# Triangular inverse of layer 0: which parts of a product are evicted and by which engine, where the memory heads stand, and where four gate panels stand

## The chip, the cores and the metric

One core of one Trainium2 chip runs the whole program. The metric is the device time of one execution in microseconds (us), the median of several. Engines in what follows: PE is TensorE (matmuls), DVE is VectorE, ACT is ScalarE, POOL is GpSimd, SP is SyncE, which only issues the loads of the weights. Each engine takes its instructions strictly in the order in which the program lists them, and waits at a semaphore when an operand isn't there yet.

## The reference, cut to what matters

Two blocks run one after the other on 256 tokens of width 1024. The change touches only layer 0 of the first block:

```python
proj = h @ a_w_in[i]                       # 29 panels of 128 columns: z, gate, q_mem, g_mem
y_br = rwkv7_time_mix(z, ...)              # 12 heads of 64, a scan over the tokens:
def step(state, inp):
    sa = jnp.einsum('bhvk,bhk->bhv', state, -kk_t)
    state = (state * w_t[:, :, None, :]
             + sa[..., None] * (kk_t * a_t)[:, :, None, :]
             + v_t[..., None] * k_t[:, :, None, :])
    y_t = jnp.einsum('bhvk,bhk->bhv', state, r_t)
def memory_cross_attention(q, mem_n, w_mem_kv):     # 4 heads of 64, 256 memory rows
    s = jnp.einsum('bshd,bmhd->bhsm', q, k) * (HEAD_DIM ** -0.5)
    p = jax.nn.softmax(s, axis=-1)
    o = jnp.einsum('bhsm,bmhd->bshd', p, v)
y = jnp.concatenate([y_br * jax.nn.silu(gate), y_mem * jax.nn.silu(g_mem)], axis=-1) @ w_out[l]
x = x + rms_norm(y, post_norm[l])
```

The rest (layer 1, two feed-forward parts, retention, sparse attention) is the same in both kernels.

## The kernel before, in words

A Python function `schedule()` writes one list of steps by hand; each engine's program walks that list and emits its own part of each step, so the order of the list is the order on every engine. Weights come as panels of 128 output columns. A panel is split into a high part (`w_hi`, ACT, line 1422) and a low part (`w_lo`, DVE, line 1758) and multiplied in 24 matmuls (lines 2281, 2282, 2284); the splits run two panels ahead of the matmuls. `between` is a list of panels and small steps from which `fill()` takes the next one at places written into the schedule. A panel's eviction is listed when the next panel is. For a gate panel the eviction is a sigmoid on ACT (line 1412) and a product on DVE (line 1819).

The scan of layer 0 is done in two chunks of 128 tokens. It needs the inverses of 24 unit triangular 128x128 matrices (12 heads, 2 chunks), kept as six groups of four. Their 32x32 diagonal blocks are inverted by substitution on DVE, one row at a time over 30 steps (`lane`, lines 1850 and 1854), after a transposition (`lanes_in`) and before another (`lanes_out`, line 1867). ACT then scatters the blocks into `xt_all` in four copies of 32 partitions (line 1524). Two levels (block sizes 32 and 64) follow for each group g, in `invert(g)`:

- `tri_1`: DVE transposes the group's diagonal blocks into `work` (line 1871)
- `tri_y`: PE multiplies (line 2339), DVE multiplies the whole 128x512 product by a mask table m5 or m6 (line 1875)
- `tri_x` (first level only) and `tri_t`: PE multiplies (line 2351), DVE adds the whole 128x512 product to the operand (lines 1881 and 1886)

`skewed` interleaves several such generators: in each round every live one makes one move, and one more joins. The groups go in two passes of three. Ahead of the first pass stand the four masked products `mat(0, "ak")` (PE line 2383, DVE line 1904); behind it `step_w(0)` (line 2400); behind the second `mat(1, "ak")`, `step_u(0)` (line 2410), and so on: state, `step_y(0)` (lines 2421, 2423), `step_w(1)` (lines 2397, 2400), `step_u(1)`, then `fill(5)` with five gate panels, `step_y(1)`, three group norms (lines 1923 to 1927), and the four memory heads. A memory head is `mem_a` (scores on PE line 2463; maximum, negation, reciprocal and two scalings on DVE lines 1934 to 1942; two exponentials on ACT line 1560), `mem_b` (four transpositions on PE line 2474, copy on ACT line 1567) and `mem_c` (two matmuls on PE line 2483, product with the gate on DVE line 1950). Its buffers lie in `xt_all`, which the inverse uses until `step_u(1)`, and its exponentials wait for `step_y(1)`. Then `branch0` splits the operands of the output projection (ACT 1580, 1583; DVE 1957) and `mix_out(0)` begins (panels `w_out`).

Of the kernel before, what the change touches and what calls it, by code (L numbers as in the profile page):

```python
# [8 lines left out]
P = 128  # L9
# [7 lines left out]
BT = BR // P  # L17
HD = 64
# [80 lines left out]
for _name, _n in VECTORS:  # L99
# [5 lines left out]
            ("dist", 384), ("mid", 2)]  # L105
TABLES_R = [(n, P) for n in ("neg_up", "m5", "m6", "up", "upinc", "cen")]
TABLES_B = [("rcos", T), ("rsin", T), ("acos", T), ("asin", T), ("icos", T), ("isin", T), ("decay", RET_HEADS * KW),
# [33 lines left out]
def const_tables():  # L141
# [10 lines left out]
    m = {"neg_up": (c > r) * -1.0, "up": (c > r) * 1.0, "upinc": (c >= r) * 1.0}  # L152
    for j in (5, 6):
        n = 1 << j
        m[f"m{j}"] = ((r // (2 * n) == c // (2 * n)) & (r // n > c // n)) * 1.0
    m["cen"] = a["ident"] - a["blkm"]
# [110 lines left out]
def build(nc, xT, memT, metaT, vecs, tab_a, tab_r, tab_b, lora, w, outT):  # L267
    with ExitStack() as ctx:
# [52 lines left out]
        xt_all = sb("xt_all", [P, 6, 512], ph)  # L321
        mrs = sb("mrs", [P, MEM], ph)
        inner = ExitStack()
        mh, ml = sb("mh", [P, KT, S], inner, F32R), sb("ml", [P, KT, S], inner, F32R)
# [18 lines left out]
        st1_flat = sqr_flat[:, 2 * BR:2 * BR + BT * HD]  # L343
        quarter = [xt_flat[:, i * 512:(i + 1) * 512].rearrange("p (a b) -> p a b", a=2) for i in range(4)]
        mp0, mpt0 = quarter[0:2], quarter[2:4]
        ybuf0 = tiles8(work_flat[:, 0:2048])
# [56 lines left out]
        def tabr(name):  # L403
            o, n = OFF_R[name]
            return tr[:, o:o + n]
# [29 lines left out]
        col_first = lambda a: a.rearrange("p a c -> p c a")  # L435

        def slot(g):
            o = 3072 + (g % 3) * 1024
            return work_flat[:, g * 512:(g + 1) * 512], work_flat[:, o:o + 512], work_flat[:, o + 512:o + 1024]
# [13 lines left out]
        def mats(c, kind, p, half):  # L453
# [22 lines left out]
            "keys_by_pool", "a_inv", "mod", "k_tilde", "bonus_r", "bonus_in", "bonus_lnb", "r_hat", "bonus_gated", "gate_scaled")  # L476
        nlt_d, ln_in, ln_m, ln, ln_out, xx_d, yy_d, xt_d = steps_of(
            "inverse_by_vector", "nlt", "lanes_in", "lane_product", "lane", "lanes_out", "x", "y", "t")
        blk_d, xts = steps_of("inverse_by_scalar", "block", "scattered")
        nl_mm, y_mm, x_mm, t_mm = steps_of("inverse_by_tensor", "l", "y", "x", "t")  # L480
# [58 lines left out]
        def schedule():  # L539
# [344 lines left out]
            def invert(g):  # L884
                do("tri_1", g)
                for level in (5, 6):
# [430 lines left out]
        def gpsimd_program(g):  # L1317
            on = Lane(g)
            for kind, *a in steps:
# [9 lines left out]
                elif kind == "zero":  # L1329
                    on.wait_ge(*in_lo.past(("h0", KT - 1)))  # L1330
                    g.memset(blocks[:, 24:BLK, :], 0.0).then_inc(*blk_zero.up(0))
                    g.memset(xt_flat, 0.0).then_inc(*xt_zero.up(0))
                elif kind == "key_b":
# [59 lines left out]
        def scalar_program(s):  # L1393
# [22 lines left out]
            for kind, *a in steps:  # L1416
# [102 lines left out]
                elif kind == "lanes_out":  # L1519
                    on.wait_ge(*ln_out.past(0))  # L1520
                    on.wait_ge(*xt_zero.past(0))
                    for r in range(P // BLK):
                        o = slice(r * BLK, (r + 1) * BLK)
                        s.activation(xt_flat.rearrange("p (m c) -> p m c", m=24)[o, :, o], blocks[o, 0:24, :],
                                     ACT.Copy).then_inc(*xts.up(r))
                elif kind == "v_tok":
# [24 lines left out]
                elif kind == "mem_a":  # L1551
# [190 lines left out]
        def vector_program(v):  # L1742
# [9 lines left out]
            for kind, *a in steps:  # L1752
# [112 lines left out]
                elif kind == "lanes_out":  # L1865
                    on.wait_ge(*ln.past(BLK - 2))
                    v.transpose(col_first(blocks), col_first(lanes)).then_inc(*ln_out.up(0))
                elif kind == "tri_1":
                    g, = a
                    on.wait_ge(*xts.past(P // BLK - 1))  # L1870
                    v.transpose(slot(g)[1], xt_all[:, g, :]).then_inc(*xx_d.up((g, 4)))
                elif kind == "tri_y":
                    g, level, b, freed = a
                    on.wait_ge(*y_mm.past((g, level)))
                    v.tensor_tensor(v4(slot(g)[2]), v4(banks[b][:, :]), b4(tabr(f"m{level}")), ALU.mult).then_inc(
                        *yy_d.up((g, level)))
                elif kind == "tri_x":
                    g, level, b, freed = a
                    xx = slot(g)[1]
                    on.wait_ge(*x_mm.past((g, level)))  # L1880
                    v.tensor_tensor(xx, xx, banks[b][:, :], ALU.add).then_inc(*xx_d.up((g, level)))
                elif kind == "tri_t":
                    g, level, b, freed = a
                    xt = xt_all[:, g, :]
                    on.wait_ge(*t_mm.past((g, level)))
                    v.tensor_tensor(xt, xt, banks[b][:, :], ALU.add).then_inc(*xt_d.up((g, level)))
                elif kind == "bonus_b":
# [5 lines left out]
                elif kind == "mat":  # L1893
# [3 lines left out]
                    if (c, which) == (0, "ak"):  # L1897
                        on.wait_ge(*xts.past(P // BLK - 1))
# [9 lines left out]
                elif kind == "state":  # L1908
                    ba, f_a, bb, f_b = a
                    on.wait_ge(*st_mm.past(0))  # L1910
                    for i in range(BT):
                        on.wait_ge(*ed_e.past(i))
                        for p in range(2):
                            o, at = HD * p, (i % 3) * P + HD * p
                            last = v.tensor_scalar(st1[o:o + HD, i, :], banks[bb if i > 2 else ba][o:o + HD, at:at + HD],
                                                   ed[o:o + HD, i, 0, CH:CH + 1], math.exp(-MID), ALU.mult, ALU.mult)
                        last.then_inc(*st_d.up(i))
# [343 lines left out]
        def tensor_program(pe):  # L2261
# [7 lines left out]
            for kind, *a in steps:  # L2269
# [71 lines left out]
                elif kind in ("tri_x", "tri_t"):  # L2341
# [3 lines left out]
                    on.wait_ge(*yy_d.past((g, level)))  # L2345
                    on.wait_ge(*(xt_d.past((g, level - 1)) if level > 5 else xts.past(P // BLK - 1)))
                    after(on, freed)
# [359 lines left out]
```

## Time and profile before

| | us |
|---|---|
| median of 3 runs | 1418.23 |
| lowest, highest | 1412.1, 1421.2 |
| the profiled execution's own time | 1421.38 |
| its span, first to last instruction | 1419.6 |

The profiled execution is another one than the three runs. What lies around its span is 1421.38 - 1419.6 = 1.8 us. The mean granted clock of TensorE over the span is 0.945 of 2.4 GHz. Read the table as the total to which savings inside the span are applied one for one, if they lie on the chain that sets the end.

### The profile page before, as it was taken

How to read it: one execution, taken by the hardware profiler on the slowest of the kernel's cores; microseconds unless marked ns; L12 is line 12 of the kernel's file. 1: busy time of each engine (PE TensorE's matmuls, PEld its weight loads, DVE VectorE, ACT ScalarE, POOL GpSimd, SP SyncE). 2: the span in 40 equal slices, each digit the busy share in tenths (PEclk: the TensorE clock that was granted, in tenths of full speed). 3: DMA queues.
4: the chain of work that ended last, by engine and by line, in shares of the span. 5: the costliest groups of instructions: out<-in, count | busy, mean ns of one | idle time of the engine just before them, and what ended most of it. 6: DMA issues, size and time to landing. Idle time of an engine off the chain costs nothing.

```text
span 1419.6 us, 23796 instructions
## 1 busy us (share of the span) xinstructions
PE 1290.4 (91%) x9682; PEld 1222.2 (86%) x9682; DVE 867.4 (61%) x1490; ACT 621.2 (44%) x1059; POOL 163.3 (12%) x165
## 2 busy tenths in 40 slices
PE   6979489968799788999998999989999998999997
PEld 6978377838689588999998999878999998999997
DVE  5668753334666557666547774657845656767652
ACT  5765101234445546444433333544344544645441
POOL 3126000400000101221002200001400000122200
PEclk9999699878899889999999999989999999999999
DMA  6433100203144236555542553324545434655561
GB/s 244 144 118 105 45 1 16 75 0 119 59 139 130 89 117 203 194 173 164 174 130 94 185 167 119 104 76 135 180 163 177 141 127 151 213 187 182 164 193 42
DMA packets 53597, 185.91 MB, mean 131 GB/s; under 512 B 6768, under 2 KB 8944, under 8 KB 53232
## 3 DMA queue, kind: packets, MB, share of 16 engines
q1 hardware_dynamic: 53056, 181.36, 39.4%
q10 hardware_dynamic: 432, 3.03, 0.6%
q8 instruction: 77, 1.26, 0.4%
q14 instruction: 32, 0.26, 0.1%
HBM read 183.32 MB, written 1.05 MB: 130 GB/s over the span
## 4 chain that ended last, share of the span: by engine, by line
PE 72%; DVE 14%; ACT 9%; issue 4%; DMA 1%; POOL 0%; DVEq 0%; ACTq 0%; POOLq 0%
PE bank L2281 19%; PE bank L2284 19%; PE bank L2282 19%; ACT wh L1422 3%; DVE wl L1758 3%; PE bank L2293 2%; PE bank L2351 1%; PE bank L2339 1%; PE bank L2266 1%; PE bank L2383 1%; DVE zl L1850 1%; PE bank L2463 1%; DVE sqr L1854 1%; PE bank L2302 1%; ACT scb L1639 1%
## 5 line engine op out<-in xcount | busy, mean ns | idle before, releaser
L2281 PE MATMUL bank<-xh,wh 128*128 128x256 f32 (+1 forms) x2008 | 588.1, 293 | 19.2 <-DVE xl L1988 10.3
L2284 PE MATMUL bank<-xh,wl 128*128 128x256 f32 (+1 forms) x2008 | 575.8, 287 | 3.6 <-DVE wl L1758 3.6
L2282 PE MATMUL bank<-xl,wh 128*128 128x256 f32 (+1 forms) x2008 | 577.3, 287 | 0.0
L1758 DVE TENSOR_TENSOR wl<-raw,wh 128x1024 fp32r<-128x1024 f32 (+1 forms) x343 | 424.1, 1241 | 232.8 <-ACT wh L1422 231.1
L1422 ACT ACTIVATE wh<-raw 128x1024 fp32r<-128x1024 f32 (+1 forms) x343 | 356.1, 1043 | 318.7 <-PE bank L2284 305.1
L2281 PEld LDWEIGHTS bank<-xh,wh 128*128 128x128 f32 x2008 | 385.5, 192 | 29.0 <-issue 18.5
L2284 PEld LDWEIGHTS bank<-xh,wl 128*128 128x128 f32 x2008 | 387.0, 193 | 4.4 <-DVE wl L1758 4.4
L2282 PEld LDWEIGHTS bank<-xl,wh 128*128 128x128 f32 x2008 | 386.2, 192 | 1.0
L1373 POOL TENSOR_TENSOR hl<-tmp,hh 128x272 fp32r<-128x272 f32 (+1 forms) x44 | 53.6, 1217 | 459.5 <-ACT hh L1672 459.5
L2281 PE MATMUL bank<-hh,wh 128*128 128x272 f32 (+1 forms) x352 | 100.3, 285 | 0.0
L2282 PE MATMUL bank<-hl,wh 128*128 128x272 f32 (+1 forms) x352 | 100.2, 285 | 0.0
L2284 PE MATMUL bank<-hh,wl 128*128 128x272 f32 (+1 forms) x352 | 100.2, 285 | 0.0
L1750 DVE TENSOR_TENSOR tmp<-bank,rstd 128x256 f32<-128x256 f32 (+1 forms) x105 | 45.1, 430 | 45.6 <-PE bank L2284 45.5
L2281 PEld LDWEIGHTS bank<-hh,wh 128*128 128x128 f32 x352 | 66.9, 190 | 0.0
L2282 PEld LDWEIGHTS bank<-hl,wh 128*128 128x128 f32 x352 | 66.5, 189 | 0.0
L2284 PEld LDWEIGHTS bank<-hh,wl 128*128 128x128 f32 x352 | 66.5, 189 | 0.0
L2281 PE MATMUL bank<-yh,wh 128*128 128x256 f32 x192 | 56.2, 293 | 3.8 <-DVE yl L2253 3.8
L2282 PE MATMUL bank<-yl,wh 128*128 128x256 f32 x192 | 54.3, 283 | 0.0
L2284 PE MATMUL bank<-yh,wl 128*128 128x256 f32 x192 | 54.3, 283 | 0.0
L2281 PEld LDWEIGHTS bank<-yh,wh 128*128 128x128 f32 x192 | 36.8, 192 | 4.6 <-DVE yl L2253 4.3
L2282 PEld LDWEIGHTS bank<-yl,wh 128*128 128x128 f32 x192 | 36.8, 191 | 0.3
L2284 PEld LDWEIGHTS bank<-yh,wl 128*128 128x128 f32 x192 | 36.7, 191 | 0.0
(345 smaller groups left out, 1627.8 us busy)
## 6 DMA issues: line engine op xcount, KB each, us to landing
raw<-w_ffn_gate SPq DMA_DIRECT2D x44, 512.0 KB, 3.5
raw<-w_ffn_up SPq DMA_DIRECT2D x44, 512.0 KB, 3.5
raw<-w_a_w_in SPq DMA_DIRECT2D x29, 512.0 KB, 3.5
raw<-w_ffn_down SPq DMA_DIRECT2D x32, 448.0 KB, 3.4
raw<-w_w_out SPq DMA_DIRECT2D x16, 512.0 KB, 3.5
raw<-w_b_w_in SPq DMA_DIRECT2D x16, 512.0 KB, 4.4
raw<-w_ffn_down SPq DMA_DIRECT2D x16, 512.0 KB, 3.5
raw<-w_ret SPq DMA_DIRECT2D x16, 512.0 KB, 3.6
```

The source lines that it names most:

```text
L1373: g.tensor_tensor(hid[n][1][:, panel, :], tmp2[t][:, 0:FFN_TOK[n]], hid[n][0][:, panel, :].bitcast(F32), ALU.subtract).then_inc(*f_lo.up(( ...
L1422: s.activation(splits[buf][0][:, 0:nk * P], raws[n % N_RAW][:, 0:nk * P], ACT.Copy).then_inc(*w_hi.up(n))
L1639: last = s.activation(scb[pb][:, c, lo:hi], scb[pb][:, c, lo:hi], ACT.Exp, bias=stb[st][:, 4 + n:5 + n], accum_out=stb[st][:, 8 + n:9 + n])
L1750: return v.tensor_tensor(out, banks[b][:, 0:n_tok], rstd[:, lo:lo + n_tok], ALU.mult)
L1758: v.tensor_tensor(lo[:, c], raws[n % N_RAW][:, c], hi[:, c].bitcast(F32), ALU.subtract).then_inc(*w_lo.up(n))
L1850: v.tensor_tensor(prod, lanes[:, 0:s, s:s + 1].broadcast_to([P, s, n]), lanes[:, s:s + 1, s + 1:BLK].broadcast_to([P, s, n]), ALU.mult).th ...
L1854: v.tensor_tensor(lanes[:, 0:s, s + 1:BLK], lanes[:, 0:s, s + 1:BLK], prod, ALU.add).then_inc(*ln.up(s))
L2266: last = pe.matmul(banks[b][:, 0:n_tok], tab(table), x, start=(k == 0), stop=(k == len(tiles) - 1))
L2281: pe.matmul(ps, hi[:, c], x_hi(k), start=(k == 0), stop=False)
L2282: pe.matmul(ps, hi[:, c], x_lo(k), start=False, stop=False)
L2284: last = pe.matmul(ps, lo[:, c], x_hi(k), start=False, stop=(k == kt - 1))
L2293: last = pe.matmul(banks[b][:, 0:n_tok], tab("ones_d"), sq_tile(k), start=(k == 0), stop=(k == KT - 1))
```

## The change

1. `tri_y` and `tri_x` evict only the blocks of the product that the level fills, as DVE copies: at the first level two of 32 partitions x 4 x 32, at the second one of 64 x 4 x 64. The mask tables m5 and m6 go. `tri_t` does the same on ACT instead of DVE.
2. Since the blocks around them must now be zero, POOL clears half of `work` too (128x3072) in step `zero`.
3. The scatter after `lanes_out` is two copies on ACT and two on DVE.
4. Memory heads of layer 0 get buffers in `ed` and `lw`; the one column of `ed` that `state` needs is copied aside first (`ed_end`, ACT). Heads 0 and 1 join the first pass of the levels, 2 and 3 the second, in `skewed`, with empty rounds between their parts.
5. `mat(0, "ak")` moves from ahead of the first pass to behind it.
6. During the lanes `fill()` is called after every step instead of four in five, and two more behind them: four gate panels that stood at `fill(5)` are now multiplied before the first pass.

```diff
+        half0 = [a.rearrange("p (a b) -> p a b", a=2) for a in (
+            ed_flat[:, 0:512], ed_flat[:, 512:1024], ed_flat[:, 1024:1536], lw[:, 0:512])]
+        mp0, mpt0 = half0[0:2], half0[2:4]
+        BELOW = {5: [(slice(32, 64), slice(0, 32)), (slice(96, 128), slice(64, 96))],
+                 6: [(slice(64, 128), slice(0, 64))]}
...
                 do("lane", s)
-                if s % 5 < 4 and len(between) > 3:
+                if len(between) > 4:
                     fill()
             do("lanes_out")
-            fill()
+            do("ed_end")
+            fill(2)
...
+            def head(h):
+                g = memory_head(0, h)
+                next(g)
+                yield
+                yield
+                next(g)
+                yield
+                yield
+                for _ in g:
+                    pass
...
+            skewed([invert(0), invert(1), invert(2), head(0), head(1)])
             masked(0, "ak")
-            skewed(invert(g) for g in range(3))
             step_w(0)
-            fill()
-            skewed(invert(g) for g in range(3, 6))
+            skewed([invert(3), invert(4), invert(5), head(2), head(3)])
             masked(1, "ak")
...
-            skewed([group_norm(j) for j in range(3)] + [memory_head(0, h) for h in range(MEM_HEADS)])
+            skewed(group_norm(j) for j in range(3))
...
+                    on.wait_ge(*rs_sum.past("mem"))
+                    g.memset(work_flat[:, 3072:6144], 0.0).then_inc(*xt_zero.up(0))
...
+                elif kind == "tri_t":
+                    g, level, b, freed = a
+                    xt = v4(xt_all[:, g, :])
+                    on.wait_ge(*t_mm.past((g, level)))
+                    for rows, cols_ in BELOW[level]:
+                        last = s.activation(xt[cols_, :, rows], v4(banks[b][:, :])[cols_, :, rows], ACT.Copy)
+                    last.then_inc(*xt_d.up((g, level)))
...
                     on.wait_ge(*mneg.past((layer, h)))
-                    on.wait_ge(*ymm.past((1, BT - 1)))
+                    if layer == 0:
+                        on.wait_ge(*ed_kept.past(0))
+                        for i in range(BT):
+                            on.wait_ge(*rhat.past(i))
+                            on.wait_ge(*ah.past(i))
...
                     on.wait_ge(*y_mm.past((g, level)))
-                    v.tensor_tensor(v4(slot(g)[2]), v4(banks[b][:, :]), b4(tabr(f"m{level}")), ALU.mult).then_inc(
-                        *yy_d.up((g, level)))
+                    for rows, cols_ in BELOW[level]:
+                        last = v.tensor_copy(v4(slot(g)[2])[rows, :, cols_], v4(banks[b][:, :])[rows, :, cols_])
+                    last.then_inc(*yy_d.up((g, level)))
```

DVE, from the last step of the lanes to the second group's transposition, before:

```order
L1854 TENSOR_TENSOR sqr<-sqr,zl 128x30
L1867 STREAM_TRANSPOSE sqr<-sqr 128x32x32
L1904 TENSOR_TENSOR sqr<-bank,tr 128x384 x4
L1871 STREAM_TRANSPOSE work<-xt_all 128x512
L1875 TENSOR_TENSOR work<-bank,tr 128x512
L1881 TENSOR_TENSOR work<-work,bank 128x512
L1886 TENSOR_TENSOR xt_all<-xt_all,bank 128x512
L1871 STREAM_TRANSPOSE work<-xt_all 128x512
```

And now, on DVE at the same place (1790 is the low part of a split, 1851 the product of a gate, 1904 the scatter, 1909 the transposition of `tri_1`):

```order
L1886 TENSOR_TENSOR sqr<-sqr,zl 128x30
L1899 STREAM_TRANSPOSE sqr<-sqr 128x32x32
L1904 COPY xt_all<-sqr 32x24x32 x2
L1790 TENSOR_TENSOR wl<-raw,wh 128x1024
L1851 TENSOR_TENSOR gate<-tmp,bank 128x256
L1790 TENSOR_TENSOR wl<-raw,wh 128x1024
L1851 TENSOR_TENSOR gate<-tmp,bank 128x256
L1909 STREAM_TRANSPOSE work<-xt_all 128x512
L1914 COPY work<-bank 32x4x32 x2
L1920 COPY work<-bank 32x4x32 x2
L1909 STREAM_TRANSPOSE work<-xt_all 128x512
```

Four masked evictions left the place ahead of the first transposition; half of the scatter, two splits and two gate products came in; of three evictions between two transpositions two are left, in halves.

DVE at the end of the first pass, before (1875, 1886 and 1881 are evictions of the levels):

```order
L1875 TENSOR_TENSOR work<-bank,tr 128x512
L1881 TENSOR_TENSOR work<-work,bank 128x512
L1886 TENSOR_TENSOR xt_all<-xt_all,bank 128x512 x2
L1875 TENSOR_TENSOR work<-bank,tr 128x512
L1886 TENSOR_TENSOR xt_all<-xt_all,bank 128x512
L1871 STREAM_TRANSPOSE work<-xt_all 128x512
```

And now (1970 to 1978 belong to `mem_a`, 1986 to `mem_c`, 1940 to `mat`):

```order
L1914 COPY work<-bank 64x4x64
L1920 COPY work<-bank 32x4x32 x2
L1970 TENSOR_REDUCE mst<-bank 128x2
L1972 TENSOR_SCALAR mst<-mst 128x2
L1975 RECIPROCAL mst<-mst 128x2
L1978 TENSOR_SCALAR ed<-ed,mst 128x256 x2
L1914 COPY work<-bank 64x4x64
L1970 TENSOR_REDUCE mst<-bank 128x2
L1972 TENSOR_SCALAR mst<-mst 128x2
L1975 RECIPROCAL mst<-mst 128x2
L1978 TENSOR_SCALAR ed<-ed,mst 128x256 x2
L1986 TENSOR_TENSOR qm<-bank,gm 64x256 x2
```

The whole softmax of head 0 now stands ahead of the last group's second-level eviction, and that of head 1 behind it.

PE at the same place, now (2388 and 2375 are products of the levels, 2500, 2511 and 2520 the three parts of a head, 2420 `mat(0, "ak")`); before, only the rows of the levels stood there, with `step_w(0)` right behind them:

```order
L2388 MATMUL bank<-xt_all,work 128x128 x4
L2500 MATMUL bank<-kmT,qm 128x256 x2
L2388 MATMUL bank<-xt_all,work 128x128 x4
L2375 MATMUL bank<-work 128x128 x4
L2500 MATMUL bank<-kmT,qm 128x256 x2
L2388 MATMUL bank<-xt_all,work 128x128 x4
L2511 MATMUL bank<-ta,ed 128x128 x8
L2520 MATMUL bank<-ed,vm 64x256 x2
L2520 MATMUL bank<-lw,vm 64x256 x2
L2420 MATMUL bank<-kkh,inv 128x128 x12
```

The scores of head 0 and of head 1 stand between products of the levels; transpositions and outputs of both heads stand behind the last one and ahead of the masked products.

## Rows read from the trace of the kernel before

**Rows 1.** The page: PE's busy tenths in 40 slices of 35.5 us.
```profile
PE   6979489968799788999998999989999998999997
```

**Rows 2.** Windows: stretch, length, busy per engine, PE clock, DMA share, GB/s.
```profile
124.70:163.50 38.80, 27.17 (x188) 25.14 (x187) 37.01 (x79) 12.18 (x19) 15.10 (x16) 0.81 0.25 82
163.50:169.70 6.20, 0.03 (x1) 0.04 (x1) 2.57 (x5) 3.85 (x5) 0.00 (x0) 0.50 0.00 0
169.70:192.70 23.00, 18.63 (x121) 17.66 (x122) 10.90 (x16) 0.00 (x0) 0.00 (x0) 0.76 0.00 1
195.60:214.70 19.10, 14.73 (x122) 13.78 (x120) 10.90 (x16) 0.78 (x2) 0.00 (x0) 1.00 0.00 1
260.00:274.40 14.40, 14.40 (x122) 14.27 (x121) 8.91 (x12) 5.33 (x8) 10.64 (x10) 1.00 0.46 147
294.70:323.00 28.30, 19.28 (x49) 10.01 (x48) 10.28 (x28) 9.34 (x25) 0.00 (x0) 0.60 0.00 1
```

**Rows 3.** Timeline, end of the lanes: start, length, engine, line, operation, count, wait.
```profile
158.22 1.22 DVE L1758 TENSOR_TENSOR wl<-raw,wh 128x1024 fp32r<-128x1024 f32 x1
163.51 3.43 ACT L1524 ACTIVATE xt_all<-sqr 32x768 f32<-32x768 f32 x4 [13.15 <-DVE sqr L1867]
167.04 1.95 DVE L1904 TENSOR_TENSOR sqr<-bank,tr 128x384 f32<-128x384 f32 x4 [3.57 <-ACT xt_all L1524]
168.91 0.70 DVE L1871 STREAM_TRANSPOSE work<-xt_all 128x512 f32<-128x512 f32 x1
```

**Rows 4.** Lines, some by form to 330 us: busy us, mean ns | idle before.
```profile
L1422 ACT ACTIVATE wh<-raw 128x1024 fp32r<-128x1024 f32 (+1 forms) x343 | 356.1, 1043 | 318.7 <-PE bank L2284 305.1
L1915 DVE TENSOR_SCALAR sqr<-bank,ed 64x64 f32<-64x64 f32 x12 | 3.4, 283 | 4.0 <-PE bank L2440 3.7
L1892 DVE TENSOR_TENSOR zk<-bank,zv 128x256 f32<-128x256 f32 x6 | 2.5, 416 | 0.0
L1399 ACT ACT_TABLE_LOAD x5 | 6.4, 1283 | 1.5 <-PE bank L2284 1.4
```

**Rows 5.** Timeline, step_w(0), the second pass and what follows it.
```profile
192.68 2.79 PE L2400 MATMUL bank<-vtok,sqr 128*128 128x128 f32 x24
...
199.57 0.69 DVE L1886 TENSOR_TENSOR xt_all<-xt_all,bank 128x512 f32<-128x512 f32 x1 [0.20 <-PE bank L2351]
200.93 2.05 PE L2339 MATMUL bank<-work 128*128 128x128 f32 x16 [1.40 <-DVE work L1871]
...
210.00 1.95 PE L2351 MATMUL bank<-xt_all,work 128*128 128x128 f32 x16
214.72 2.60 PE L2383 MATMUL bank<-kkh,inv 64*128 64x128 f32 x24
217.25 2.89 PE L2410 MATMUL bank<-wu_w,xt_all 128*128 128x128 f32 x24
```

**Rows 6.** Timeline, from the first memory head to the first panel of w_out.
```profile
298.28 0.68 DVE L1934 TENSOR_REDUCE mst<-bank 128x2 f32<-128x512 f32 x1
301.12 1.11 PE L2474 MATMUL bank<-ta,xt_all 128*128 128x128 f32 x4 [5.27 <-DVE xt_all L1942]
307.13 1.11 PE L2474 MATMUL bank<-ta,xt_all 128*128 128x128 f32 x4 [0.99 <-DVE xt_all L1942]
323.41 1.90 DVE L1957 TENSOR_TENSOR xl<-zv,xh 128x512 fp32r<-128x512 f32 x3
324.25 0.55 PE L2281 MATMUL bank<-xh,wh 128*128 128x256 f32 x1 [1.34 <-DVE xl L1957]
```

**Rows 7.** Timeline, POOL's clearing; the same DVE form beside POOL and alone.
```profile
120.11 2.66 POOL L1332 MEMSET xt_all<- 128x3072 f32 x1
130.08 0.68 DVE L1854 TENSOR_TENSOR sqr<-sqr,zl 128x58 f32<-128x58 f32 x1
160.77 0.22 DVE L1854 TENSOR_TENSOR sqr<-sqr,zl 128x58 f32<-128x58 f32 x1
```

More of the change, by code:

```diff
@@ L322, in build @@
         mrs = sb("mrs", [P, MEM], ph)
+        ed_end = sb("ed_end", [P, BT], ph)
         inner = ExitStack()
@@ L1521, in scalar_program @@
                     on.wait_ge(*xt_zero.past(0))
-                    for r in range(P // BLK):
+                    for r in (0, 1):
                         o = slice(r * BLK, (r + 1) * BLK)
-                        s.activation(xt_flat.rearrange("p (m c) -> p m c", m=24)[o, :, o], blocks[o, 0:24, :],
-                                     ACT.Copy).then_inc(*xts.up(r))
+                        s.activation(by_block[o, :, o], blocks[o, 0:24, :], ACT.Copy).then_inc(*xts.up(r))
+                elif kind == "ed_end":
+                    for i in range(BT):
+                        on.wait_ge(*ed_e.past(i))
+                    s.activation(ed_end[:, :], ed[:, :, 0, CH:CH + 1], ACT.Copy).then_inc(*ed_kept.up(0))
+                elif kind == "tri_t":
[5 more added lines that the diff above has]
+                    last.then_inc(*xt_d.up((g, level)))
                 elif kind == "v_tok":
@@ L1556, in scalar_program @@
                     on.wait_ge(*mneg.past((layer, h)))
-                    on.wait_ge(*ymm.past((1, BT - 1)))
+                    if layer == 0:
+                        on.wait_ge(*ed_kept.past(0))
+                        for i in range(BT):
+                            on.wait_ge(*rhat.past(i))
+                            on.wait_ge(*ah.past(i))
                     after(on, f_p)
@@ L1867, in vector_program @@
                     v.transpose(col_first(blocks), col_first(lanes)).then_inc(*ln_out.up(0))
+                    on.wait_ge(*ln_out.past(0))
+                    on.wait_ge(*xt_zero.past(0))
+                    for r in (2, 3):
+                        o = slice(r * BLK, (r + 1) * BLK)
+                        v.tensor_copy(by_block[o, :, o], blocks[o, 0:24, :]).then_inc(*xts_v.up(r))
                 elif kind == "tri_1":
                     g, = a
-                    on.wait_ge(*xts.past(P // BLK - 1))
+                    on.wait_ge(*xts.past(1))
+                    on.wait_ge(*xts_v.past(3))
                     v.transpose(slot(g)[1], xt_all[:, g, :]).then_inc(*xx_d.up((g, 4)))
@@ L1874, in vector_program @@
                     on.wait_ge(*y_mm.past((g, level)))
-                    v.tensor_tensor(v4(slot(g)[2]), v4(banks[b][:, :]), b4(tabr(f"m{level}")), ALU.mult).then_inc(
-                        *yy_d.up((g, level)))
+                    for rows, cols_ in BELOW[level]:
+                        last = v.tensor_copy(v4(slot(g)[2])[rows, :, cols_], v4(banks[b][:, :])[rows, :, cols_])
+                    last.then_inc(*yy_d.up((g, level)))
                 elif kind == "tri_x":
                     g, level, b, freed = a
-                    xx = slot(g)[1]
                     on.wait_ge(*x_mm.past((g, level)))
[L1881 to L1886, printed above, removed]
+                    for rows, cols_ in BELOW[level]:
+                        last = v.tensor_copy(v4(slot(g)[1])[rows, :, cols_], v4(banks[b][:, :])[rows, :, cols_])
+                    last.then_inc(*xx_d.up((g, level)))
                 elif kind == "bonus_b":
@@ L2345, in tensor_program @@
                     on.wait_ge(*yy_d.past((g, level)))
-                    on.wait_ge(*(xt_d.past((g, level - 1)) if level > 5 else xts.past(P // BLK - 1)))
+                    on.wait_ge(*(xt_d.past((g, 5)) if level > 5 else xts.past(1)))
+                    on.wait_ge(*xts_v.past(3))
                     after(on, freed)
```

24 lines of the change are left out of this document (11 added, 13 removed).

## The prediction

> **What bounds the kernel now.** I began with the page's row of PE in 40 slices [rows 1]. PE shows 8 or 9 tenths nearly everywhere; the hole is in slices 5 to 10, some 140 to 355 us, which is layer 0. There the kernel waits on chains that go from engine to engine. Next I cut that stretch into windows by stage [rows 2]. In the lanes (124.7 to 163.5 us) DVE is busy 37.0 of 38.8 us: DVE sets the time, and PE has 11.6 us of holes. From 163.5 to 169.7 PE does nothing while the blocks are scattered and four masked products are evicted. The first pass of the levels takes 23.0 us at a mean clock of 0.76, the second 19.1 us at 1.00; PE is busy 14.7 us of the latter. Five gate panels then take 14.4 us of pure PE time at 260 us, and the four memory heads take 28.3 us at a clock of 0.60, with no engine busy in full. The timeline shows why [rows 6]: one head's transpositions follow another's by 6.01 us (301.12 to 307.13), a round trip through all three engines. The timeline also names the waits inside a pass [rows 5]: PE waits 1.40 us for the next group's transposition, which DVE does only after it has evicted two products.
>
> **The change, part by part.** All sums go by the profiled execution, 1421.4 us. It is 3.2 us above the median of the three runs, so I take the saving off both.
>
> *The heads leave the tail.* The last group norm ends on DVE when head 0's maximum begins, at 298.3 [rows 6]. Behind it, without heads, stands only the split of the first operand, a third of the 1.90 us of three; ACT's part of it can be done beside the norms. So the first w_out panel starts at 298.3 + 0.6 + 0.1 = 299.0 instead of 324.25: -25.2. This part is the safest: all that stood there is listed elsewhere now, nothing new stands in its place. That panel began at the half clock in the trace (heads' window 0.60) and would now follow the norms closely. A panel takes 14.4/5 = 2.9 us at the full clock; at half it is up to twice that. I take -1.3 as half of it, with ends 0 and -2.9.
>
> *Four gate panels leave 260 us:* 4/5 of 14.4 = -11.5. Their matmuls lie in the lanes and up to the first transposition, where PE has 11.6 + 6.2 us free [rows 2], so I cost them at nothing there. One panel still covers the evictions behind `step_u(1)`. If PE were at the half clock there the four would take up to 23 us, and some of it would stick out; that is in the range. Their DVE and ACT parts are not free.
>
> *From the lanes to the first transposition* DVE sets the time, so what it gets counts. Two more splits and two more products lie inside the lanes: 2 x (1.2 + 0.4) = +3.2 [rows 3, 4]. The scatter falls from four copies on ACT (3.43) to two with DVE's two beside them: -1.7. The masked evictions go from here: -1.9. Ahead of the transposition now stand two more splits, and the first waits for its high part, which ACT starts only after the scatter and the copy of a column (0.2, an estimate from the smallest ACT and DVE rows): 0.2 + 1.04 + (1.2 + 0.4) x 2 = +4.4, the second high part lying beside the first low one. Together +4.0. This wait is the one thing the move adds: queued behind it on DVE is the transposition, and PE waits for that. Bounds: +2 if DVE's two scatter copies and the high part come early, +6 if the high part waits for its buffer, which the matmuls of the panel before must free.
>
> *POOL clears twice as much*, 2.66 us more, and three gates' work of POOL moves into lanes and levels. The row beside POOL took 0.68, the same alone 0.22 [rows 7]. The bonus work that is pushed back has its taker later. I take +0.5, ends 0 and +2.
>
> *The levels.* No row shows a copy of 32 x 128 from a bank. The nearest are 64 x 64 at 283 ns and 128 x 256 at 416 ns [rows 4]; I take 0.25 each, so two are 0.5 against 0.69, and one 64 x 256 is 0.4. Taking `tri_t` off DVE saves another 0.6 ahead of each next transposition. Per pass, two such gaps: 2 x (0.2 + 0.2 + 0.6) = -2.0. PE's own products at 0.9 us a group of four (two in 1.95) set the rest. In the second pass the last first-level product began at 210.00, 14.4 us in [rows 5]; now 12.4.
>
> From there the heads decide. All times from the pass's start: that product ends at 13.3; scores of head 0 reach DVE at 14.4; the softmax takes 2.84 (298.28 to 301.12, DVE held from the first maximum to the last scaling, as it waits inside for ACT's exponentials): 17.2. Only then comes the last group's second-level eviction, 17.6, then head 1's softmax, 20.4, whose end PE needs for the transposition, 21.0; ACT's copy, 21.7; two outputs on PE in order, 22.8. Then come 24 masked matmuls, 2.6: 25.4, and behind the first pass `step_w(0)`, 2.8: 28.2. Before, pass and `step_w(0)` took 23.0 + 2.9 = 25.9. Of that, 23.0 - 19.1 = 3.9 was the slow clock at its start. PE would again be idle some 5 us before the first pass (last gate panel done about 168, transposition about 173 + 0.7), and in the trace the clock stood at 0.50 after such a gap [rows 2]. So I keep the 3.9: 28.2 + 3.9 - 25.9 = +6.2. Second pass until `step_u(0)`: 25.4 against 217.25 - 195.6 = 21.6: +3.8. Bounds for both together: +1 (clock warm, heads' waits shorter) to +16 (next paragraph but one).
>
> Of the extra switches of ACT's table, one comes ahead of head 0's exponentials: 1.28 us [rows 4], beside DVE's maximum and negation (0.9) and behind an eviction; it costs 0.1 to 0.5 and is in the bound. The other lies ahead of a gate's sigmoid, with ACT idle. The Trainium skill, in "ScalarE: Activation LUTs", section "What ACT_TABLE_LOAD costs", speaks against this part of the change: it puts every switch at about 2.66 us with the drain, and its section "Table sets: the hidden batching unit" says to batch calls by set. By its figure the first pass would be longer by about 1.4 us more, an estimate; the load alone in this trace agrees with its 1283 ns, and no row shows the drain.
>
> **Sum:** -25.2 - 1.3 - 11.5 + 4.0 + 0.5 + 6.2 + 3.8 = -23.5. That is 1398 for the profiled execution and 1418.2 - 23.5 = 1394.7 for the median: **1395 us**.
>
> **The rivals.**
>
> *Warm clock and heads well hidden.* If the gate panels keep PE busy up to the first pass, the 3.9 us go; and if the softmax in the levels takes less of DVE than 2.84, because ACT's part overlaps, each pass gives about 2 more. -23.5 - 3.9 - 4 = -31.4: 1387. For it: PE is idle only between panels. Against it: DVE holds the panels apart, since each waits for its low part, and the clock fell in the lanes too (mean 0.81).
>
> *Heads as serial inside as outside.* Both engines are in order, and ACT's evictions of `tri_t` stand between two heads' exponentials, so DVE waits for ACT, ACT for DVE, PE for both. Then a head costs its 6.01 us in the levels as well. A pass without heads would be 19.1 - 2.0 - 0.3 = 16.8; with two at 6.0 it is 28.8 instead of 22.8: +12 over both. -11.5: 1407. Against it: groups give PE work meanwhile.
>
> *The gate panels do not fit.* The change would not do what it says: moved ahead of the levels at half clock, they take 23 us instead of 11.5, 17.8 of it free. 5 us stick out, and the high part waits with them, +4: 1404.
>
> *Slower than before.* The mechanism is TensorE's clock in the levels. In the trace it was 1.00 from the second pass on with PE busy 77% of it; with heads in between, as in the heads' own window (0.60, PE busy 68% although at half clock), it may stay low from the first pass to `step_y(0)`. The PE time there at the full clock is 14.7 + 14.7 + 2.9 x 3 + 2.6 x 3, about 46 us. At half, with a third of it hidden in waits, it adds 30: -23.5 + 30: 1425. It decides from about 24 us more, so half the clock for half of this stretch is not enough.
>
> [...]
>
> **How the numbers follow.** Chances: forecast, 1390 to 1400, 0.45; warm and hidden 0.25; serial 0.14; panels don't fit 0.09; slower 0.04; 0.03 for none of these. Changes of under about 1% (14 us) can't be told from none, so faster means below 1404. Forecast and warm case are there in full, the panels' case half, the serial one a fifth: 0.78 with a little more for mixtures: 0.82. Within 1% gets 0.14, slower by over 1% gets 0.04. The range goes from 1384 (the warm case with its cheaper bounds) to 1407 (the serial one). It leaves out the slower case and half of the serial one.
>
> **What would show it.** Right: no memory head behind the group norms, w_out's first panel within 1.5 us of their end; one gate panel ahead of `step_y(1)`; DVE's first `tri_1` at about 173; `step_u(0)` at about 231 instead of 217; a slow clock at the first pass's start. Wrong: PE at half clock past 190; heads further than 6 us apart inside a pass; gate panels later than the first transposition.

## The result and the profile after

The changed kernel takes 1398.44 us (median of 4 runs, 1391.87 to 1400.84), the kernel before 1419.41 in the runs beside it: ratio 0.9843, 95% interval 0.9817 to 0.9869. The forecast was 1395, range 1384 to 1407. The profiled execution took 1397.52 us (span 1395.7), 23.9 less than that of before.

The page's row of PE in 40 slices of 34.9 us, which answers to [rows 1]; the granted clock of the changed kernel stands below it. Slice 5 (140 to 175 us, the end of the lanes and the start of the levels) has risen from 4 to 6 tenths. The hole in which the heads stood (slice 9) stands at 7 instead of 6, and slice 10 at 7 instead of 8:
```profile
PE   6988689977799689999998999889999998999997
PEclk9999899798999699999999999989999999999999
```

Windows of the changed kernel by stage, columns as in [rows 2]: the lanes; from there to the first product; first pass; second pass; the second call of `step_w`; the two groups of PE work behind it; w_out's first panel.
```profile
124.70:166.90 42.20, 34.78 (x234) 33.02 (x233) 40.49 (x83) 14.58 (x25) 20.17 (x21) 0.84 0.31 100
166.90:173.50 6.60, 0.58 (x5) 0.38 (x4) 4.75 (x7) 4.33 (x7) 1.94 (x2) 0.91 0.21 65
173.50:201.10 27.60, 24.68 (x169) 21.56 (x169) 11.78 (x32) 6.90 (x20) 4.10 (x5) 0.90 0.07 24
203.80:226.90 23.10, 19.79 (x147) 16.94 (x145) 9.89 (x28) 6.11 (x20) 0.00 (x0) 1.00 0.00 1
248.40:261.10 12.70, 12.70 (x50) 9.11 (x48) 0.00 (x0) 0.77 (x2) 0.00 (x0) 0.73 0.00 0
261.10:271.20 10.10, 10.10 (x49) 9.70 (x48) 2.23 (x4) 0.98 (x2) 0.00 (x0) 0.50 0.01 2
301.50:305.00 3.50, 3.48 (x16) 3.50 (x17) 2.81 (x4) 1.40 (x2) 0.00 (x0) 0.50 0.00 0
```
PE stands still ahead of the levels for 6.05 us (its row below). In the kernel before it was longer than the 6.2 us of the window in [rows 2]:
```profile
169.67 2.08 PE L2339 MATMUL bank<-work 128*128 128x128 f32 x8 [9.45 <-DVE work L1871]
```
The clock ahead of the pass is now 0.91 instead of 0.50. In the kernel before it had stood at half since 150 us (0.51 in the window from 150 to 151, 0.50 from 156 to 160 with PE busy) and came back at about 181. In the changed kernel PE has panels to do up to 167.5 us, and the clock falls at 172 and is back at about 179. Over the pass it is 0.90 instead of 0.76. The pass is longer all the same, since two heads are in it.

Timeline of DVE from the end of the lanes to the first product's eviction, which answers to [rows 3]:
```profile
164.63 2.25 DVE L1899 STREAM_TRANSPOSE sqr<-sqr 128x1024 f32<-128x1024 f32 x1
166.91 1.14 DVE L1904 COPY xt_all<-sqr 32x768 f32<-32x768 f32 x2
169.83 1.22 DVE L1790 TENSOR_TENSOR wl<-raw,wh 128x1024 fp32r<-128x1024 f32 x1 [1.79 <-ACT wh L1440]
...
171.30 1.22 DVE L1790 TENSOR_TENSOR wl<-raw,wh 128x1024 fp32r<-128x1024 f32 x1
...
172.77 0.70 DVE L1909 STREAM_TRANSPOSE work<-xt_all 128x512 f32<-128x512 f32 x1
175.64 0.59 DVE L1914 COPY work<-bank 32x128 f32<-32x128 f32 x2 [2.17 <-PE bank L2375]
```
Behind each of the two splits stands a gate product of 0.41, not shown. DVE waits 1.79 us for ACT's high part of a weight panel, and the transposition is queued behind it. It starts at 172.77; before, at 168.91.

The levels on PE with the heads in them, which answers to [rows 5], both passes:
```profile
173.53 2.07 PE L2375 MATMUL bank<-work 128*128 128x128 f32 x8 [6.05 <-DVE work L1909]
...
196.20 0.66 PE L2511 MATMUL bank<-ta,ed 128*128 128x128 f32 x4 [1.23 <-DVE ed L1978]
196.79 1.08 PE L2520 MATMUL bank<-ed,vm 128*64 128x256 f32 x4
...
198.55 2.60 PE L2420 MATMUL bank<-kkh,inv 64*128 64x128 f32 x24
201.08 2.89 PE L2437 MATMUL bank<-vtok,sqr 128*128 128x128 f32 x24
203.81 1.11 PE L2375 MATMUL bank<-work 128*128 128x128 f32 x8
...
208.20 2.05 PE L2375 MATMUL bank<-work 128*128 128x128 f32 x16 [0.54 <-DVE work L1909]
...
226.95 2.60 PE L2420 MATMUL bank<-kkh,inv 64*128 64x128 f32 x24
229.48 2.89 PE L2447 MATMUL bank<-wu_w,xt_all 128*128 128x128 f32 x24
```
PE's wait for the next group's transposition fell from 1.40 to 0.54. The end of a pass belongs to the heads: PE waits for head 1's scaling (1.23) and then does its transposition and both outputs. `step_u(0)` (229.48) began at 217.25 before.

And the end of the part, timeline, which answers to [rows 6]:
```profile
300.08 0.69 DVE L1963 TENSOR_TENSOR zv<-zv,zk 128x512 f32<-128x512 f32 x1
300.69 1.89 DVE L1993 TENSOR_TENSOR xl<-zv,xh 128x512 fp32r<-128x512 f32 x3
301.52 0.55 PE L2317 MATMUL bank<-xh,wh 128*128 128x256 f32 x1 [4.30 <-DVE xl L1993]
```
w_out's panel follows the last norm directly, 22.7 us earlier in the program than before (324.25).

### The profile page after: what moved, and what is told of

Read it like the earlier page. It is cut to its first block, busy times and chain, and to the rows that moved or that the text cites. A ratio compares the mean times of both kernels' runs of the same rounds, so it can differ in the third digit from the quotient of the medians.

```text
span 1395.7 us, 23837 instructions
## 1 busy us (share of the span) xinstructions
PE 1281.3 (92%) x9682; PEld 1218.8 (87%) x9682; DVE 858.1 (61%) x1492; ACT 626.5 (45%) x1078; POOL 165.1 (12%) x166
## 4 chain that ended last, share of the span: by engine, by line
PE 72%; DVE 14%; ACT 9%; issue 4%; DMA 1%; POOL 1%; DVEq 0%; ACTq 0%; POOLq 0%
PE bank L2317 19%; PE bank L2320 19%; PE bank L2318 19%; DVE wl L1790 3%; ACT wh L1440 3%; PE bank L2329 2%; PE bank L2420 1%; PE bank L2302 1%; PE bank L2375 1%; DVE zl L1882 1%; PE bank L2388 1%; DVE sqr L1886 1%; PE bank L2338 1%; ACT scb L1671 1%; PE bank L2437 1%
```

## The experiments

The first three runs take the prediction's sum apart, part by part; the others try what the profile after suggested. All times below are to be read against 1398.4 us of the changed kernel (4 runs; the kernel before took 1419.5 to 1420.2 in the sessions of the experiments, 1419.4 in that one); "first product" is the row at 173.53 there, "`step_u(0)`" 229.48 and "end of norms" 300.69.

**The heads back behind the norms.**
```diff
-            skewed([invert(0), invert(1), invert(2), head(0), head(1)])
+            skewed(invert(g) for g in range(3))
...
-            skewed([invert(3), invert(4), invert(5), head(2), head(3)])
+            skewed(invert(g) for g in range(3, 6))
...
-            skewed(group_norm(j) for j in range(3))
+            skewed([group_norm(j) for j in range(3)] + [memory_head(0, h) for h in range(MEM_HEADS)])
```


> The changed kernel with the four memory heads back behind the group norms (buffers and waits stay as changed). My theory: w_out's first panel starts 25.1 us later after the norms' end, but each pass of the levels loses the stretch that the heads hold it, from 22.8 to 16.8 us until its last product, so 12 us come back: +13, about 1411. Rival 1, the levels hide the heads entirely: +25, about 1423. Rival 2, the heads cost inside what they cost outside: no change, about 1398.

Measured: 1410.66 us (10 runs), ratio to before 0.9942 (0.9923 to 0.9962), 12.2 above the changed kernel. PE's timeline of this run:
```profile
198.03 1.11 PE L2375 MATMUL bank<-work 128*128 128x128 f32 x8
...
214.96 2.60 PE L2420 MATMUL bank<-kkh,inv 64*128 64x128 f32 x24
217.50 2.89 PE L2447 MATMUL bank<-wu_w,xt_all 128*128 128x128 f32 x24
```
The second pass up to its masked products takes 214.96 - 198.03 = 16.9 us, with two heads in it 226.95 - 203.81 = 23.1. With `step_u(0)` as the end it is 6.2 us in both passes. So a head costs 3.1 us in the levels and 25.1 / 4 = 6.3 behind them, and the heads' move brings 12 to 13 us of the 21.

**The gate panels back behind step_w(0).**
```diff
-                if len(between) > 4:
+                if s % 5 < 4 and len(between) > 3:
...
-            fill(2)
+            fill()
+            settle()
...
             step_w(0)
+            fill()
```


> The changed kernel with the fills of the kernel before (four gate panels back at 260 us; the last gate of the memory heads is evicted ahead of the levels, as they need it). My theory: +11.5 for the panels, -3.2 for the splits and products that leave the lanes, -3.3 for the queue ahead of the first transposition, and the half clock of the middle stretch 1.7 shorter as before: +3 to +5, about 1402. Rival, that the panels are hidden in full where they stand now: +11.5, about 1410. Rival, that they only moved: 1398.

Measured: 1403.5 us (4 runs), ratio 0.9884 (0.985 to 0.9919), 5.1 above. The first product starts at 168.46 (5.1 earlier), `step_u(0)` at 224.69 (4.8 earlier), the end of norms is 5.0 later. So the early panels cost 4.8 and save 9.8.

**The levels alone**: both edits above and `mat(0, "ak")` ahead of the first pass again. What is left of the change are the copies, `tri_t` on ACT, the halved scatter and the clearing.

> The kernel before with the part on evictions alone: blocks as copies, the products of T on ScalarE, half of the scatter on VectorE, the larger clearing; heads, gate panels and masked products stand as before. My theory: -1.7 for the scatter and -2.3 in each pass: 6 us under the kernel before, about 1413. Rival, that smaller copies save nothing since TensorE's products set the pace: -2, about 1417. Rival, that they are what carries the whole change: 1398.

Measured: 1415.78 us (10 runs), ratio 0.9955 (0.993 to 0.998). The first product starts at 168.30 (before 169.67), the second pass lasts 19.4 us to `step_u(0)` instead of 21.6 [rows 5], the first with `step_w(0)` 22.1 instead of 26.0. So the levels gain 2.2 us in each pass, and the first some more by its clock, at half for some 7 us of it instead of 11. The profiled execution took 1410.97 us, 4.8 less than the median of these runs (1407.0 to 1417.4), so its stages show more than the median does: that one is 4.4 us below the kernel before, where 6 were expected.

The three parts add up in the medians: 12.2 for the heads, 5.1 for the panels and 4.4 for the levels are 21.7, against 21.0 of the whole change. The place of the masked products, the part not counted here, has a run of its own below.

**The two softmaxes of a pass as a pair.** In the changed kernel DVE stands still between a head's negation and its reciprocal, since ACT's exponentials are between them. The DVE rows of the changed kernel:
```profile
190.05 0.69 DVE L1970 TENSOR_REDUCE mst<-bank 128x2 f32<-128x512 f32 x1 [1.36 <-PE bank L2500]
190.78 0.17 DVE L1972 TENSOR_SCALAR mst<-mst 128x2 f32<-128x2 f32 x1
192.04 0.17 DVE L1975 RECIPROCAL mst<-mst 128x2 f32<-128x2 f32 x1 [1.09 <-ACT ed L1592]
192.24 0.62 DVE L1978 TENSOR_SCALAR ed<-ed,mst 128x256 f32<-128x256 f32 x2
```
The edit puts reciprocal and scaling into a step of its own, behind the other head's maximum:
```diff
+                if layer == 0:
+                    yield
+                do("mem_n", layer, h, p, st)
...
+                for row in ((0,), (0, 1), (0, 1, 2), (0, 1, 2, "a", "b"), (1, "a", 2), (2, "b", "a", "b", "a", "b")):
+                    for k in row:
+                        next(m0 if k == "a" else m1 if k == "b" else inv_[k], None)
```


> The changed kernel with the softmaxes of two heads interleaved: both maxima ahead of both reciprocals on VectorE, and the last group's eviction between them. My theory, that VectorE held inside two serial softmaxes of 2.84 us sets the end of each pass: 1.9 us less per pass, 3.8 in all, about 1394.5. Rival, that TensorE's own products set that end: no change, 1398.

Measured: 1394.23 us (4 runs), ratio 0.9821 (0.9778 to 0.9863), 4.2 below. DVE of this run:
```profile
190.34 0.69 DVE L1969 TENSOR_REDUCE mst<-bank 128x2 f32<-128x512 f32 x1 [1.36 <-PE bank L2502]
191.07 0.17 DVE L1971 TENSOR_SCALAR mst<-mst 128x2 f32<-128x2 f32 x1
191.14 0.69 DVE L1969 TENSOR_REDUCE mst<-bank 128x2 f32<-128x512 f32 x1
...
192.32 0.17 DVE L1977 RECIPROCAL mst<-mst 128x2 f32<-128x2 f32 x1 [0.29 <-ACT ed L1591]
```
The wait of 1.09 is 0.29, and the pass with `step_w(0)` is 1.4 us shorter, the second 1.4: 2.8 in the profile instead of the 3.8 expected. The median's 4.2 is more than the stages account for, and the span of the profiled execution is only 1.3 shorter. The interval of the ratio overlaps with that of the changed kernel (0.9817 to 0.9869), and so do those of the next two single edits, so the size of each rests on its stages as much as on its median.

**The first transposition ahead of the panels.**
```diff
+            do("tri_1", 0)
+            depth[0] = 1
             fill(2)
+            depth[0] = N_SPLIT
+            split_hi()
+            split_hi()
...
-                do("tri_1", g)
+                if g:
+                    do("tri_1", g)
+                if g in (1, 2):
+                    split_lo()
```


> The changed kernel with the first group's transposition put ahead of the two fills of the projection panels on TensorE, and with the splits of those panels on VectorE (two of the first half, then the second halves) put behind the transposed copies of the first two groups instead of ahead of the first. Theory one, the +3.9 us between the end of the lanes and the first transposed copy is work queued ahead of it on VectorE and TensorE, which nothing needs yet: the first y product starts at about 169.4 us instead of 173.5, and the clock has no time to fall in the first pass (-1.9), against +0.5 of the deferred work: about -5.5 in all, 1393. Theory two, the deferred splits are wanted inside the first pass, and its products wait for VectorE there as long as they waited ahead of it: 1398, no change.

Measured: 1393.25 us (4 runs), ratio 0.982 (0.9796 to 0.9845), 5.2 below. PE and its window in this run:
```profile
171.34 1.16 PE L2383 MATMUL bank<-work 128*128 128x128 f32 x8 [2.02 <-DVE work L1917]
```
```profile
171.30:200.00 28.70, 25.26 (x192) 22.05 (x192) 16.30 (x38) 9.30 (x24) 5.99 (x6) 1.00 0.11 37
```
The time is as the first theory had it, and so is the clock: 1.00 over the whole pass, which with `step_w(0)` takes 28.7 instead of 30.3. The start isn't: 171.3, not 169.4, since the last step of the lanes got a panel's split beside it and ended 1.9 us later (its transposition at 166.56 instead of 164.63). The deferred splits cost nothing visible in the pass.

**step_w(1) in two loops.** Its products with the state have 64 rows, those with the masked matrices 128, and they take turns. Changed kernel, PE, at the full clock and at half:
```profile
250.94 0.48 PE L2434 MATMUL bank<-sqr,kkh 64*128 64x128 f32 x2
251.36 0.49 PE L2437 MATMUL bank<-vtok,work 128*128 128x128 f32 x2
...
257.05 0.79 PE L2434 MATMUL bank<-sqr,kkh 64*128 64x128 f32 x2
257.77 0.79 PE L2437 MATMUL bank<-vtok,work 128*128 128x128 f32 x2
```
Each fp32 product of the program is two MATMUL records in the trace, and prices here are per record. Two of a kind start 0.42 us ahead of the next two: 0.21 each, while `step_w(0)`, all of 128 rows, does 24 in 2.7 us (201.08 to 203.81), 0.114 each, and `mat(0, "ak")`, all of 64, does 24 in 2.5. The edit:
```diff
+                    if c:
+                        on.wait_ge(*st_d.past(BT - 1))
+                        for i in range(BT):
+                            pe.matmul(banks[b][:, i * HD:(i + 1) * HD], kk[o:o + HD, i, CH:2 * CH],
+                                      st1_flat[o:o + HD, i * HD:(i + 1) * HD], start=(i == 0), stop=False)
                     for i in range(BT):
-                        n = min(P, (BT - i) * HD)
+                        n = HD if c else min(P, (BT - i) * HD)
...
-                        last = pe.matmul(out, mat(c, "ak", p, i), vtok[:, c, h * HD:h * HD + n], start=not c, stop=True)
+                        last = pe.matmul(out, mat(c, "ak", p, i), vtok[:, c, h * HD:h * HD + n], start=not c,
+                                         stop=not c or i == BT - 1)
```


> The changed kernel with the second call of step_w written as two loops, all products with the state first and then all products with the masked matrices, in place of one loop that takes them in turn (64 and 128 rows). Theory one, the stretch of matmuls of changing height is where TensorE is granted half its clock while it is busy all the time: the stretch at half clock (17 us in the changed kernel, 250 to 271 us) goes, and with it 7 to 12 us: about 1388. Theory two, the stretch is of something else (the load of all engines, the number of columns that stream), and stays: 5 us less at most, 1393 to 1398.

Measured: 1391.62 us (6 runs), ratio 0.9809 (0.9785 to 0.9834), 6.8 below. PE's rows and windows of this run:
```profile
251.33 1.55 PE L2431 MATMUL bank<-sqr,kkh 64*128 64x64 f32 x12
252.81 1.55 PE L2438 MATMUL bank<-vtok,work 128*128 128x64 f32 x12
```
```profile
251.30:257.20 5.90, 5.90 (x49) 5.65 (x48) 0.00 (x0) 0.77 (x2) 0.00 (x0) 1.00 0.00 0
257.20:261.70 4.50, 4.50 (x26) 4.22 (x24) 1.67 (x3) 0.49 (x1) 0.00 (x0) 0.54 0.01 4
```
The stage falls from 12.7 to 5.9 us, 0.123 a record, at the full clock. The stretch at half clock doesn't go: it moves to the matmuls behind, where it now lasts some 7 us instead of 17, with a second short one ahead of the stage (0.56 from 247 to 250). The gain, 6.8, lies just under the 7 to 12 of the first theory and above the 5 that the second allowed at most; the first theory's claim on the clock is half true. At the full clock alone 48 records of 0.21 would be 10.0 us, so of the 6.8 that the stage lost some 4.1 are the lower price and 2.7 the clock that did not fall inside it (an estimate from these rows).

**The same products narrow, but still in turn.** The run before changed order and width at once.
```diff
-                        n = min(P, (BT - i) * HD)
+                        n = HD if c else min(P, (BT - i) * HD)
```


> The changed kernel with the products of step_w's second call 64 columns wide instead of up to 128, and still in the one loop that takes 64 and 128 rows in turn. It tells apart the two things that the run with two loops changed at once. Theory one, the turn from 64 to 128 rows is what costs: 0.18 us a product as in the two 64-column pairs of the changed kernel's trace (0.36 us each for two products) against 0.208, so 48 x 0.028 = -1.3 us, and the stretch at half clock stays: 1396 to 1398. Theory two, the columns cost: the stretch comes to the 5.9 us of the run with two loops, and with it -5 to -7: 1392.

Measured: 1399.15 us (4 runs), ratio 0.9853 (0.9827 to 0.9878): nothing gained. PE's rows:
```profile
251.32 0.43 PE L2437 MATMUL bank<-vtok,work 128*128 128x64 f32 x2
251.69 0.43 PE L2434 MATMUL bank<-sqr,kkh 64*128 64x64 f32 x2
```
0.18 a record in turn against 0.123 in a row, at the same width, height and clock. The stage takes 10.9 us (250.23 to 261.18) and falls to half clock as before, at 255.9. It starts later than in the changed kernel by 1.8 us, of which 1.2 are from a dip of the clock ahead of it (0.51 from 246 to 249, as in the run with two loops), and this eats the 1.8 that it is shorter. By the stages the columns bring 1.8 us and the order 5.0 (10.9 to 5.9). Of these 5.0, 48 x 0.06 = 2.9 are the lower price, an estimate; the rest is that the clock fell behind the stage instead of in it. So the order is most of what the two loops brought.

The two loops change one thing more: where each product of a pair used to start a sum that the next one finished in the same place, now one start serves a whole bank. That alone isn't what costs. The products of `state` start and finish sums in the same way, in turn, and all have 128 rows:
```profile
237.80 0.39 PE L2476 MATMUL bank<-wu_u,btok 128*128 128x128 f32 x2
238.02 0.39 PE L2477 MATMUL bank<-vtok,ktok 128*128 128x128 f32 x2
```
They cost 0.11 each. What is left, of the things that these runs vary, is the height that changes.

**The masked products ahead of the first pass.**
```diff
+            masked(0, "ak")
             skewed([invert(0), invert(1), invert(2), head(0), head(1)])
-            masked(0, "ak")
```


> The changed kernel with the four masked matrices of chunk 0 written ahead of the first pass of levels again, as before the change (1.95 us on VectorE ahead of the first transposed copy), instead of behind it, where step_w waited for them at most 2.7 us. Theory one: +1.95 ahead and -2.6 at the end of the pass, so no change that can be measured, 1397 to 1398. Theory two, TensorE's clock falls further for the 2 us more of idle time ahead of the pass: +2, 1400.

Measured: 1397.01 us (4 runs), ratio 0.9852 (0.9826 to 0.9877): no change. The first product starts 2.4 later (175.98), `step_w(0)` 0.6 later: where this step stands makes no difference that these runs can show.

**Two and three together.** The three gains are the pair, the transposition and the loops.

> The changed kernel with three edits at once: each head's scaled copies directly after its softmax's sum (the pair of the earlier run), the first group's transposition ahead of the panels, and step_w's second call in two loops. If the gains add (-3.8, -5.5, -7 to -12): 1377 to 1382. If the half clock in the middle stays: about 1389. If the first pass is bound by the same VectorE queue in both first edits, one of them brings nothing: 4 to 5 more than these.

Measured: 1385.18 us (4 runs), ratio 0.9766 (0.9742 to 0.979), 13.3 below the changed kernel. That is short of the 1377 to 1382 of full addition and better than 1389. The single gains were 4.2, 5.2 and 6.8, 16.2 in all; in the profiled spans they were 1.3, 3.4 and 5.1, and together 14.0. The sum is 2.9 too high in the medians and 4.2 too low in the spans, so they add to within 3 to 4 us. Windows of this run, from the lanes' end to the first product, the first pass, and the stretch at half clock in the middle:
```profile
167.60:170.10 2.50, 0.24 (x3) 0.03 (x1) 1.86 (x4) 2.45 (x6) 0.00 (x0) 1.00 0.03 13
170.10:199.20 29.10, 26.27 (x192) 24.03 (x193) 15.75 (x38) 9.28 (x23) 5.14 (x6) 0.88 0.11 37
247.00:256.00 9.00, 9.00 (x53) 8.71 (x54) 2.23 (x4) 0.82 (x2) 0.00 (x0) 0.62 0.01 2
```


> The changed kernel with the softmax pair and step_w's second call in two loops, without the transposition put first: if what that edit brought holds in company (-5.2 alone in the medians, -3.4 in the profiled executions), this is 3 to 5 us above the kernel with all three (1385.2): 1388 to 1390. If it brings nothing beside the other two: 1385.

Measured: 1388.33 us (4 runs), ratio 0.978 (0.9758 to 0.9801): 3.2 above the three, and each of its runs (1388.2 to 1392.3) lies above each of theirs (1383.5 to 1386.4). The transposition put first is worth its place in company as well. With all three the kernel is faster than either of the two kernels compared here.

## Why the prediction was right

All stages by the profiled executions, one of each kernel, before against after:

| step | forecast | measured |
|---|---|---|
| from the lanes to the first product, POOL with it | +4.5 | +3.9 (169.67 to 173.53) |
| first pass and `step_w(0)` | +6.2 | +4.3 (26.0 to 30.3) |
| second pass | +3.8 | +4.1 (21.6 to 25.7) |
| `step_u(0)` to the end of norms, four gate panels fewer | -11.5 | -9.8 (81.0 to 71.2) |
| heads behind the norms, and w_out's panel | -26.5 | -25.1 |
| the rest of the program | 0 | -1.2 |
| sum | -23.5 | -23.9 |

The forecast was within 0.4 us of the profiled executions. The medians fell by less, 21.0 us (the interval of the ratio allows 19 to 26), which is why 1398.4 stands against the 1395 forecast; both are in the range. The parts that carried the sum, the tail, the panels and what two heads cost inside a pass, came as described, and the experiments show each by itself. The clock terms did not.

*The tail* went as forecast (-25.1 against -25.2). The term of -1.3 for a warmer first panel of w_out did not come: PE has idled 4.3 us ahead of it, and the window at 301.5 still shows 0.50.

*The gate panels* took 11.4 us out (14.4 to 3.0). The stretch at half clock ahead of their old place, 13.5 us long before (242 to 255.5) and 17 in the changed kernel (254 to 271), gave 1.6 back. The forecast had no such term; I had read the stretch of before as given.

*Ahead of the first transposition* the list of what DVE does was right to 0.6 us, and the wait for the high part was the one named (1.79 us in the trace).

*The passes.* The forecast of a pass without heads, 16.8, stands at 16.9 in the run with the heads late, and that of two heads in it, +6.0, at 6.2 in both. A softmax holds DVE 2.81 us as forecast (2.84). The copies of 32 x 128 take 0.30 each, not 0.25. The step that was mis-sized is the slow clock at the start of the first pass, taken over as 3.9: to the masked products the first pass takes 25.0 and the second 23.1, so it was 1.9. The prediction kept the 3.9 because in the trace "the clock stood at 0.50 after such a gap", and that reading of the trace was wrong: the gap was 9.45 us and not some 6, and the clock had been at half for 20 us when that pass began, so the rows could not show what a gap of 6 us at the full clock costs. In the changed kernel the clock fell at 172 us, 4.8 us after the last panel, and was back at about 179. That is a half of the rival with the warm clock. With the transposition put first the pass and `step_w(0)` took 1.5 less at a clock of 1.00, most of the rest.

*The table of ACT.* The timeline of the changed kernel:
```profile
189.00 0.55 ACT L1552 ACTIVATE xt_all<-bank 32x128 f32<-32x128 f32 x2 [2.30 <-PE bank L2388]
189.56 1.28 ACT L1417 ACT_TABLE_LOAD   x1
190.98 0.47 ACT L1592 ACTIVATE ed<-bank,mst 128x256 f32<-128x256 f32 x1
```
It is loaded at 189.56 for 1.28 us and hidden: the exponential starts at 190.98, 0.03 after the maximum's negation on DVE (190.78 + 0.17) that it needs. The Trainium skill, "ScalarE: Activation LUTs", section "What ACT_TABLE_LOAD costs", would have had 2.66 us with the drain; ACT's last row ahead of the load ends at 189.55 and its next starts 0.14 after it, so no drain of that size is in this trace, and the measurement decides.

*The rivals.* Serial heads are out: 3.1 us a head, not 6.0. The panels did fit: PE was through with them at 167.5. The half clock through the levels is out: 1.00 in the second pass, with PE's waits in it. There the gaps were of 1.3 us and less. The Trainium skill, "TensorE: Matmul & The Clock Gate", section "Why this matters for your kernels", ties the loss of the clock to long idle gaps. The trace agrees in the first pass, whose half clock follows 6.05 us without a matmul, and in the second, which kept 1.00; that gives no account of `step_w(1)`, where the clock fell with PE busy all the time.

Part of the match is luck, errors that cancel. The result was worse than forecast by 1.3 of clock at the end and 1.7 in the middle, and better by 1.9 of clock at the start, by 0.6 ahead of the first product, and by 1.2 in code that wasn't touched, for which the forecast had no term and the runs no cause.

## What to carry to other kernels

Work that waits on round trips through three engines is cheap where another such chain already leaves holes: four heads cost 3.1 us each between the levels and 6.3 behind them. Price what is then queued ahead of the first instruction that others wait for, and put that one first; it was 3 to 5 us here. And look at stretches in which TensorE is busy in full as closely as at those with waits: of the edits tried on the changed kernel, the one on the order of matmuls of two heights gained the most, 6.8 us.

## What the runs showed of the hardware

- fp32 matmuls of 64 and of 128 rows that take turns cost 0.18 us a record at the full clock and 64 columns; twelve of one height after another cost 0.123. At 128 columns it is 0.21 in turn, 0.105 for 24 of 64 rows one after another and 0.114 for 24 of 128. So among matmuls of one height the narrower ones are no cheaper here.
- TensorE's granted clock fell from 1.00 to 0.50 in a stretch in which PE was busy 12.7 of 12.7 us (`step_w(1)`), in the kernel before too (12.5 of 12.5). In two loops the stretch at half clock became shorter and came elsewhere. Turns of 64 and 128 rows do not bring it about by themselves: `step_y(1)` takes such turns too, and the changed kernel kept 1.00 in it with PE busy 11.0 of 11.0 us (window from 277 to 288). What does stays open.
- The run with the transposition first kept the clock at 1.00 through the first pass after 2.02 us without a matmul; the one with three edits had 2.27 us, and the clock fell as the pass began (0.50 from 171 us, 0.88 over the pass). Why these differ is open as well.
